# Feed-forward up projection on the un-normed residual, with the shift as two more columns and the square sums on GpSimd

## What is computed

```python
lat = lat + g1 * yl
hl = modulate(rmsnorm(lat, norm_g[l, 1]), sh2, sc2)
lat = lat + g2 * conv_ffn(hl, ffn_w_up[l], ffn_conv_w[l], ffn_conv_b[l], ffn_w_down[l])

def conv_ffn(h, w_up, conv_w, conv_b, w_down):
    u = dwconv(h @ w_up, conv_w, conv_b)
    gate, val = jnp.split(u, 2, axis=-1)
    return (jax.nn.silu(gate) * val) @ w_down
```

## Time and profile before

| what | value |
|---|---|
| median of 3 runs | 873.41 us (873.29 to 873.53) |
| span of the profiled execution | 873.0 us; no other time is given for it |
| TensorE busy | 861.6 us, 99% of the span |
| weight load busy | 781.1 us, 89% |
| DVE busy | 643.3 us, 74% |
| ACT busy | 488.7 us, 56% |
| GpSimd busy | 0.2 us |
| mean granted TensorE clock | 0.998 of full speed |

### The profile page before, as it was taken

The page is one execution under the profiler, slowest core; times in us unless marked ns, Lnnn a source line. Parts: engine busy times, 40 slices in busy tenths (PEclk is TensorE's granted clock), DMA queues, the critical chain, the costliest instruction groups (busy, mean ns, idle before and its releaser), DMA issues.

```text
span 873.0 us, 16978 instructions
## 1 busy us (share of the span) xinstructions
PE 861.6 (99%) x6294; PEld 781.1 (89%) x6294; DVE 643.3 (74%) x1086; ACT 488.7 (56%) x774; POOL 0.2 (0%) x4
## 2 busy tenths in 40 slices
PE   8999999999999999999999999999999999999997
PEld 3688888888899999999998899999998899999996
DVE  4783899999997787777668797766578765555555
ACT  5434677777766654555557545555544654444443
POOL 0000000000000000000000000000000000000000
PEclk9999999999999999999999999999999999999999
DMA  9974444444445556565564654444465465555551
GB/s 344 408 297 145 151 144 146 148 145 147 156 166 221 193 214 214 176 218 191 169 194 142 198 188 148 155 158 146 145 220 172 141 208 194 178 191 191 176 186 48
DMA packets 45441, 160.90 MB, mean 184 GB/s; under 512 B 5200, under 2 KB 6608, under 8 KB 45264
## 3 DMA queue, kind: packets, MB, share of 16 engines
q1 hardware_dynamic: 43488, 156.43, 51.5%
q10 hardware_dynamic: 1904, 3.81, 1.2%
HBM read 159.16 MB, written 1.05 MB: 184 GB/s over the span
## 4 chain that ended last, share of the span: by engine, by line
PE 88%; DVE 5%; DMA 2%; ACT 2%; issue 1%; SPq 1%; DVEq 0%; ACTq 0%
PE bank L417 20%; PE bank L419 20%; PE bank L418 19%; PE bank L471 5%; PE bank L472 5%; PE bank L473 5%; DVE w_lo L411 2%; PE bank L1220 2%; PE bank L1224 2%; PE bank L1228 2%; DMA arena<-in_ada 1%; ACT w_hi L404 1%; PE bank L439 1%; DMA raw<-in_stream 1%; PE bank L1346 1%
## 5 line engine op out<-in xcount | busy, mean ns | idle before, releaser
L411 DVE TENSOR_TENSOR w_lo<-raw,w_hi 128x1024 fp32r<-128x1024 f32 x244 | 294.9, 1222 | 117.4 <-ACT w_hi L404 117.1
L417 PE MATMUL bank<-h_hi,w_hi 128*128 128x256 f32 (+1 forms) x1168 | 349.0, 299 | 1.0 <-DVE w_lo L411 1.0
L419 PE MATMUL bank<-h_hi,w_lo 128*128 128x256 f32 (+1 forms) x1168 | 344.0, 295 | 0.0
L418 PE MATMUL bank<-h_lo,w_hi 128*128 128x256 f32 (+1 forms) x1168 | 343.3, 294 | 0.0
L404 ACT ACTIVATE w_hi<-raw 128x1024 fp32r<-128x1024 f32 x244 | 252.8, 1051 | 106.8 <-PE bank L419 82.0
L417 PEld LDWEIGHTS bank<-h_hi,w_hi 128*128 128x128 f32 x1168 | 219.6, 188 | 10.8 <-issue 1.3
L418 PEld LDWEIGHTS bank<-h_lo,w_hi 128*128 128x128 f32 x1168 | 220.6, 189 | 6.5
L419 PEld LDWEIGHTS bank<-h_hi,w_lo 128*128 128x128 f32 x1168 | 219.7, 188 | 5.7
L417 PE MATMUL bank<-y_hi,w_hi 128*128 128x256 f32 x304 | 86.9, 286 | 0.1
L419 PE MATMUL bank<-y_hi,w_lo 128*128 128x256 f32 x304 | 85.9, 283 | 0.0
L418 PE MATMUL bank<-y_lo,w_hi 128*128 128x256 f32 x304 | 85.3, 281 | 0.0
(11 more groups left out here) (278 smaller groups left out, 1098.2 us busy)
## 6 DMA issues: line engine op xcount, KB each, us to landing
raw<-in_stream SPq DMA_DIRECT2D x244, 512.0 KB, 3.3
arena<-in_ada SPq DMA_DIRECT2D x40, 512.0 KB, 7.3
xres<-in_ada SPq DMA_DIRECT2D x8, 512.0 KB, 3.2
tok<-in_tok SPq DMA_DIRECT2D x4, 512.0 KB, 5.6
con<-in_con ACTq DMA_DIRECT2D x1, 1472.0 KB, 6.2
xres<-in_tok ACTq DMA_DIRECT2D x1, 1024.0 KB, 8.6
out<-arena SPq DMA_DIRECT2D x4, 256.0 KB, 2.0
arena<-in_post_mix ACTq DMA_DIRECT2D x1, 512.0 KB, 4.3
```

The lines of the kernel that those rows point to most:

```text
L411: dve.tensor_tensor(w_lo[c.slot][:, :], raw[c.slot][:, :], w_hi[c.slot][:, :].bitcast(F32), ALU.subtract).then_inc(S("split_lo"), 1)
L417: pe.matmul(dst, hi_w, a_hi, start=start, stop=False, skip_group_check=True)
L418: pe.matmul(dst, hi_w, a_lo, start=False, stop=False, skip_group_check=True)
L419: return pe.matmul(dst, lo_w, a_hi, start=False, stop=stop, skip_group_check=True)
```

## The change

1. The up projection multiplies the residual times `gain_2` (no root, no shift). `scaled_hi` and `scaled_lo`, which the second block's input used already, now take a gain and a width, and make `h_hi` and `h_lo` straight from `xres`.
2. Each tile of `h_hi` and `h_lo` is 258 wide (FW): behind the 256 tokens stand two columns with the shift (`shift_columns`), so column 256 of the product is the shift times the weights. Every up matmul has 258 columns.
3. The root is applied to the product. `ffn_scaled` (DVE) multiplies the bank by `rstd`, 257 columns, into a new SBUF tile `z_f`; `ffn_middle` (ACT) adds column 256 as a bias in place, then makes the middle tap; the taps (`ffn_taps`) read `z_f`. The bank is free after `ffn_scaled`.
4. All eight squares are added on GpSimd (seven adds), and TensorE makes one float32 matmul (`squares_sum`) inside chunk 51. `norm_sum`, `pair_squares`, `keep_clock`'s eight matmuls, `norm_input` and `split_h_hi` go.
5. The sum of g2's tiles moves from DVE to GpSimd: a multiplication and, from the second tile on, an addition, each 128x1024.
6. Chunks 48 to 51 are now value 0, gate 1, gate 0, value 1; and the steps of a tile on ACT and DVE are spread between the chunks' `hi` and `lo`.

```diff
-GATE_ROWS = (0, 0, 1, 1, 1, 1, 1, 1, 1, 1)
+FW = T + 2
...
+        def squares_sum(pe, bank):
+            pe.wait_ge(S("squares_added"), QUARTERS + KT - 1)
+            pe.matmul(psum[bank][:, 0:T], ones, wide[:, 0:T], start=True, stop=True).then_inc(S("norm_summed"), 1)
...
-        def scaled_hi(act, update, m):
+        def scaled_hi(act, update, m, gain, width):
             wait_residual(act, update, m)
-            act.activation(h_hi[:, x], xres[:, x], ACT.Copy, scale=final_pre[:, m:m + 1]).then_inc(S("h_hi"), 1)
+            act.activation(h_hi[:, m * width:m * width + T], xres[:, m * T:m * T + T], ACT.Copy,
+                           scale=gain[:, m:m + 1]).then_inc(S("h_hi"), 1)
...
             hi(act, Chunk(N_FFN, 1))
+            hi(act, Chunk(N_FFN, 2))
+            for m in range(KT):
+                scaled_hi(act, 0, m, gain_2, FW)
+            hi(act, Chunk(N_FFN, 3))
             square_residual(act, 0)
-            hi(act, Chunk(N_FFN, AHEAD))
-            norm_rstd(act, 0, 1)
-            split_h_hi(act, 1, lambda m: mod[:, 3 * KT + m:3 * KT + m + 1])
+            hi(act, Chunk(N_FFN, 4))
+            hi(act, Chunk(N_FFN, 5))
+            norm_rstd(act, 0, 1, bank=3)
...
-                    act.activation(conv[p][half], psum[4 + 2 * half + p][:, 0:T], ACT.Identity,
+                    act.wait_ge(S("z"), t * 2 + (1 + half))
+                    z = z_f[p][half]
+                    act.activation(z[:, 0:T], z[:, 0:T], ACT.Identity, bias=z[:, T:T + 1]).then_inc(S("z_full"), 1)
+                for half in range(2):
+                    act.wait_ge(S("z_full"), t * 2 + (1 + half))
+                    act.activation(conv[p][half], z_f[p][half][:, 0:T], ACT.Identity,
...
-            norm_sum(pe)
-            keep_clock(pe, HOUT_BANKS[0], IDLE)
+            pe.wait_ge(S("mod_rows"), QUARTERS + 3)
+            pe.wait_ge(S("final_weights"), 3)
+            first_columns_late(pe, [Chunk(N_FFN), Chunk(N_FFN, 1)], [psum[6][:, 0:FW], psum[5][:, 0:FW]], 2 * KT, FW)
+            pe.wait_ge(S("residual"), KT)
+            column_tile(pe, Chunk(N_FFN, 2), psum[4][:, 0:FW], FW, FW)
+            column_tile(pe, Chunk(N_FFN, 3), psum[7][:, 0:FW], FW, FW, lambda: squares_sum(pe, 3), 1)
+
+            def ffn_up(j, p, c):
+                pe.wait_ge(S("z"), j * 2 - 2)
+                column_tile(pe, c[0], psum[4 + p][:, 0:FW], FW, FW)
+                column_tile(pe, c[1], psum[6 + p][:, 0:FW], FW, FW)
...
+        @block.gpsimd
+        def _(pool):
+            for n, (to, by) in enumerate(((0, 1), (2, 3), (4, 5), (6, 7), (0, 2), (4, 6), (0, 4))):
+                if n < 4:
+                    pool.wait_ge(S("norm_squares"), by + 1)
+                else:
+                    pool.wait_ge(S("squares_added"), QUARTERS + (2, 4, 6)[n - 4])
+                x = wide[:, to * T:to * T + T]
+                pool.tensor_tensor(x, x, wide[:, by * T:by * T + T], ALU.add).then_inc(S("squares_added"), 1)
+            for k in range(KT):
+                pool.wait_ge(S(f"mod_loaded{k % 4}"), 16 * (k // 4 + 3))
+                c_k = cs[:, 2 * k:2 * k + 1]
+                if k == 0:
+                    pool.tensor_scalar(gate_sum, gate_raw[0], c_k, None, ALU.mult).then_inc(S("gate_summed"), 1)
+                else:
+                    x = gate_raw[k % 4]
+                    pool.tensor_scalar(x, x, c_k, None, ALU.mult).then_inc(S("gate_scaled"), 1)
+                    pool.wait_ge(S("gate_summed"), k)
+                    pool.wait_ge(S("gate_scaled"), k)
+                    pool.tensor_tensor(gate_sum, x, gate_sum, ALU.add).then_inc(S("gate_summed"), 1)
...
             add_product(dve, lambda m: mod[:, 2 * KT + m:2 * KT + m + 1], 0, N_FFN, HOUT_BANKS)
-            pair_squares(dve)
-            lo(dve, Chunk(N_FFN, AHEAD))
+            for m in range(KT):
+                scaled_lo(dve, 1, m, gain_2, FW)
+            for k in range(2, 6):
+                lo(dve, Chunk(N_FFN, k))
...
-            norm_input(dve, 1, lambda m: gain_2[:, m:m + 1], lambda m: mod[:, 3 * KT + m:3 * KT + m + 1])
+            def ffn_scaled(t, p, n_done):
+                dve.wait_ge(S("multiplied"), n_done)
                 for half in range(2):
+                    dve.tensor_tensor(z_f[p][half][:, 0:T + 1], psum[4 + 2 * half + p][:, 0:T + 1], rstd[:, 0:T + 1], ALU.mult).then_inc(S("z"), 1)
```

More of the change, by code:

```diff
@@ L116, in constants @@
     return c, m.reshape(P, 2 * P)
-IDLE = 8
 WARM = 6
@@ L307, in build @@
         m_relu = [part(T) for _ in range(2)]
-        used[0] = 4096
+        z_f = [[part(FW) for _ in range(2)] for _ in range(2)]
+        used[0] = 4112
         gate_sum = part(D)
@@ L429, in column_tile, with first_columns_late @@
             last.then_inc(S("multiplied"), 1)
-        def first_columns_late(pe, chunks, dsts, input_tiles):
+        def first_columns_late(pe, chunks, dsts, input_tiles, width=T):
             for c in chunks:
@@ L438, in first_columns_late @@
                     for w in (w_hi, w_lo):
-                        pe.matmul(dst, w[c.slot][:, k * P:k * P + P], h_hi[:, k * T:k * T + T], start=k == 0 and w is w_hi,
+                        pe.matmul(dst, w[c.slot][:, k * P:k * P + P], h_hi[:, k * width:(k + 1) * width], start=k == 0 and w is w_hi,
                                   stop=False, skip_group_check=True)
@@ L443, in first_columns_late @@
                 for c, dst in zip(chunks, dsts):
-                    last = pe.matmul(dst, w_hi[c.slot][:, k * P:k * P + P], h_lo[:, k * T:k * T + T], start=False,
+                    last = pe.matmul(dst, w_hi[c.slot][:, k * P:k * P + P], h_lo[:, k * width:(k + 1) * width], start=False,
                                      stop=k == KT - 1, skip_group_check=True)
@@ L959, in _ @@
             hi(act, Chunk(N_HOUT, 7))
+            act.wait_ge(S("mod_all"), 1)
+            act.activation(shift_columns(h_hi), shifts, ACT.Copy).then_inc(S("mod_rows"), 1)
             out_squares(HEADS - 1, 1)
@@ L2009, in _ @@
             lo(dve, Chunk(N_HOUT, 7))
+            dve.wait_ge(S("mod_rows"), QUARTERS + 3)
+            dve.tensor_tensor(shift_columns(h_lo), shifts, shift_columns(h_hi).bitcast(F32), ALU.subtract).then_inc(S("final_weights"), 1)
             out_gated(HEADS - 1, 1)
@@ L2038, in ffn_tile, with ffn_lo @@
                 dve.tensor_tensor(u_f[p], f_silu[p], conv[p][1], ALU.mult).then_inc(S("u_full"), 1)
-                if between is not None:
-                    between()
+            def ffn_lo(t, p, s):
                 dve.wait_ge(S("u_hi"), t + 1)
```

149 lines of the change are left out of this document (64 added, 85 removed).

## The result

| | median of its runs, us | profiled span, us |
|---|---|---|
| before | 873.4 (873.3 to 873.5) | 873.0 |
| changed | 886.19 (885.91 to 886.61) | 884.1 |

The ratio is 1.0148, 95% interval 1.0136 to 1.016. The change costs 12.8 us where 4.5 us of gain were forecast: it is slower, and outside the range given. By that, the profiled execution of 873.0 would have taken some 874.8 us (an estimate), 1.4 above the median.

The account below looks back on a forecast made before the run. TensorE, busy 99% of the span, was taken as the bound. Terms -4.3 - 1.0 + 0.8 = -4.5 us took the span from 873.0 to 868.5, the time to 868.9; own range 868.0 to 870.9, whole range up to 879.5.

Parts of the forecast that it names:

- The entry: Start of the up projection on TensorE: first chunk pair from 271.84 instead of 277.00, 5.2 us earlier.
- Two more columns: Up matmuls of 258 instead of 256 columns: 0.95 us more TensorE time, 0.8 of it counted in the sum.
- rival C: Up matmuls: columns past 256 cost the fixed 5 ns again, 5.3 us in all, 874.2 us; chance 0.03.
- Rival D: Entry: late h_hi tiles or banks keep some of the 5.2 us gap, 871 to 873 us; chance 0.05.
- Rival B: First down projection waits for tile 0 behind slow GpSimd adds, over 1 us each: 871.1 us; chance 0.09.
- The stall: TensorE's wait for a chunk near 335, behind SP's held stream: 1.0 us, expected to go.
- The 0.4 us between span and median: Added to the forecast span of 868.5 to get the time, as the runs' median lay 0.4 above the span.
- rival A: GpSimd ops reading SBUF and DVE ops with two SBUF tensors block each other: +8.5 us, 877.4; chance 0.37.
- First down projection: Tile 0's chain through GpSimd's squares: sum ready at 280.5, first down projection at 290.05, 4.3 us earlier.
- Gate sums: Moving DVE's eight gate passes to GpSimd: nothing by itself, but the 1.0 us stall near 335 goes.
- Cover in each tile: DVE and ACT chain per tile: 8.0 us against TensorE's 8.66, hiding scalings and ACT's passes with 0.6 to spare.

Follow-up runs that it names:

- e6_gap: e3 with VectorE's gate pass moved from behind the activations' low half to right behind the gated product; GpSimd empty: 870.23 us (0.9961).
- e5: The kernel before, unchanged, executed and profiled once more: 873.96 us, with a span of 872.2 us.
- e1: The changed kernel with the gate sums back on DVE at their old place, the squares' additions still on GpSimd: 879.82 us (1.0075).
- e3: The changed kernel with both squares' additions and gate sums on DVE, gate sums at their old place, GpSimd empty: 875.54 us (1.0029).
- e2: The changed kernel with the seven squares' additions on DVE, the gate sums still on GpSimd: 882.31 us (1.0111).
- e4: The kernel before with only its gate sums moved to GpSimd: 882.98 us (1.0114).
- e10: The changed kernel with 18 idle float32 matmuls on TensorE ahead of its wait for the sum of squares: 886.12 us (1.0148).
- e7: e6_gap with 40 idle 128x1024 memsets, which only write, on the empty GpSimd: 870.24 us (0.9962).
- e8: e6_gap with 14 idle 128x1024 multiplications by a column on the empty GpSimd: 873.59 us (1.0006).

## Why the prediction failed

**What held.** *The entry*: TensorE starts at 271.88 (forecast 271.84), chunk 50 at 277.67 (277.64), and in e6_gap, where GpSimd disturbs nothing, the time is 870.2 against 868.9. *Two more columns*: a tile in e6_gap takes 8.63 us with 48 matmuls of 258 columns, and rival C's step of 5 ns on each would show as 0.24 us, so rival C is out. *Rival D* is out by the entry's stamps. *Rival B* is out as a cause by itself: a GpSimd addition alone takes 0.72 us, 1.7 times DVE's 0.42 and inside the bounds 0.42 to 0.84.

That 870.2 lies near 868.9 is in part luck, as the sum was -4.3 - 1.0 + 0.8. In e6_gap the first down projection comes 3.5 us earlier and not 4.3, and the tile behind it takes 0.2 more. The stall, counted at 1.0, was worth nothing: the second trace of the kernel before hasn't got it (e5). The two columns, counted at 0.8, cost nothing, 8.63 us a tile against 8.64 before. The last miss hides part of the others, and the gain in time is 3.2 us where 4.5 were forecast. The 0.4 us between span and median was a misreading too: it compared the span of one execution with the times of others.

**The step that failed** is the choice between the forecast and rival A, and it stood in *First down projection* and *Gate sums*. In the first, the squares' additions were taken as 0.63 us each one after another, ready at 280.5. They took 9.97 us in all and ended at 285.44, where rival A's sum had put 285.4, and TensorE waited 4.0 us for them; on GpSimd they cost 4.3 us (e1 less e3). In the second, "DVE loses eight passes ... nothing by itself" set the price of moving them to GpSimd at nothing; it was 6.4 us against DVE doing them at their old place (the changed kernel less e1), some 12 against DVE doing them in its gap (e2 less e6_gap), and 9.6 in the kernel before (e4). The evidence that I counted against A, that nothing in the trace spoke for it, was none, as GpSimd was idle in that trace and couldn't have shown it; and the Trainium skill (SBUF — State Buffer, Who interferes with whom), cited there, stated the lock outright.

**Rival A's price was too low as well**, 877.4 with a dear end of 882 against 886.2, and the runs show two sizes and a term left out:
- *The durations.* The multiplication was taken as 1.1 us, 1.5 times a DVE row; it takes 2.85 alone, 3.8 times DVE's 0.75. The 1024-wide addition was taken as 1.85 and takes 2.44. The first four gate sums thus last from 285.4 to 305.0, twice the "some 10 us" of the sum, and lie on tiles 0 to 2.
- *The hold.* "A GpSimd op slips in and costs about 0.9 each" fits the multiplications, 0.8 at most, but an addition holds DVE for what is left of it, 1.6 us at 291.97 and 2.2 at 302.66.
- *The clock*, which was in no sum: behind the two long waits it fell to half. e10 shows that for the first of them this cost nothing beyond the wait of the chain beside it; the second was not tried.

**The gate sums' place** was in no term. In the step *Cover in each tile* the chain was found 8.0 us with 0.6 to spare; measured 8.1. Its consequence was not drawn: a gate pass of 1.3 us left on DVE at its old place would exceed the cover. e3 shows up to 0.7 us per such tile, 5.3 in all (e3 less e6_gap). So in this order the passes did have to leave DVE's chain, but not DVE: 1.43 us in each tile stood open (e6). The chain had been summed link by link, without asking where in it DVE itself stands idle.

**The stall near 335** The earlier trace rows is gone in e6_gap, and there the fourth gate sum on DVE ends at 319.5 instead of 325.0, so that SP goes on with the stream 5.5 us sooner. But that is no gain in the usual time, as the kernel before showed the stall in one of its two traces only.

By differences of runs, then: without GpSimd's work and with the passes in the gap, 870.2; the squares on GpSimd 4.3 (e1 less e3); the gate sums there 12.1 (e2 less e6_gap). The sum is 886.6; measured 886.2. That the parts nearly add up is no proof of each, since in e2 the first four gate sums meet the entry. Against e6_gap, the change's order with all elementwise work on DVE is a gain of 3.2 us, and the use of GpSimd for squares and gate sums a loss of 16.0.

## What to carry to other kernels

Elementwise work on GpSimd was not free even where nobody waited for it: beside a VectorE whose operations have two SBUF inputs, each GpSimd addition of two SBUF tensors held VectorE for the rest of its own length, and GpSimd's own operations were held while VectorE had no gap. Before moving work off VectorE, look for the gap that VectorE has inside each period: its timeline showed 1.4 us, and a pass put there cost nothing. Where GpSimd must be used, operations that only write were free here, and cutting additions short gave back 4.9 us. A wait seen in one trace may belong to that execution alone: hold it against a second one, and its span against the usual spans, before counting on it. And a trace in which an engine is idle is no evidence against a conflict with it.

## What the runs showed of the hardware that was not expected

- On GpSimd a multiplication of one 128x1024 float32 tensor by a column takes 2.85 us, longer than the sum of two such tensors, 2.44 us; a 128x256 sum takes 0.72 us and a 128x1024 memset 0.95.
- The multiplication is slower and yet the milder neighbour: 14 of them cost 3.4 us, 14 additions 26.9 us, 40 memsets nothing.
- VectorE's operations with a bank and one SBUF tensor kept 408 to 427 ns beside all of it. Its multiplication of a 128x1024 tensor by a column, with one SBUF input, took 1.19 us instead of 0.75 beside the memsets (e7) and 1.52 beside the multiplications (e8).
- TensorE's granted clock was 0.50 after 4.0 us without matmuls, from 286 to 290, and idle matmuls in that wait kept it at 1.00, for no gain in time (e10). In e10 TensorE then stood 3.0 us up to 297.01, and the clock stayed at 1.00 from 296 to 302; it was 0.50 from 304 to 306, behind a second wait of 2.6 us.
